# Attention scores over all 128 rows: high and low query halves stacked, or one half beside zeros

## Time and profile before

| What | Value |
|---|---|
| Timed executions | 2894.48, 2897.59, 2910.16 us |
| Profiled execution | 2885.39 us |
| its span | 2883.8 us |
| PE busy | 2633.6 us, 91% |
| PE weight loads | 2125.8 us, 74% |
| DVE busy | 1583.0 us, 55% |
| ACT busy | 1130.1 us, 39% |
| POOL busy | 184.0 us, 6% |
| mean granted TensorE clock | 0.931 |

### The profile page before, as it was taken

How to read it: one execution, slowest core, us unless ns; L and a number is a source line. 1 busy time by engine, 2 the same in 40 slices (tenths; PEclk the granted TensorE clock), 3 DMA queues, 4 the chain that set the end, 5 groups by cost and what they waited for, 6 DMA issues and landing times.

```text
span 2883.8 us, 42857 instructions
## 1 busy us (share of the span) xinstructions
PE 2633.6 (91%) x13598; PEld 2125.8 (74%) x13598; DVE 1583.0 (55%) x3532; ACT 1130.1 (39%) x2388; POOL 184.0 (6%) x221
## 2 busy tenths in 40 slices
PE   1899999989999889999969999998999998799997
PEld 1677777778777667888858677786887786588886
DVE  3456775667266555554244677565745647555522
ACT  1224545354354443222222455453634444322222
POOL 3300000000000220000030000000000011200000
PEclk8979999999999959999987999998999996899998
DMA  4511111212313212333341111122132141133332
GB/s 77 131 30 38 30 45 53 62 55 59 87 45 103 82 29 73 95 96 96 93 108 52 38 38 30 52 59 52 52 88 59 48 135 30 51 95 95 94 99 70
DMA packets 343966, 196.35 MB, mean 68 GB/s; under 512 B 29340, under 2 KB 338704, under 8 KB 343152
## 3 DMA queue, kind: packets, MB, share of 16 engines
q1 hardware_dynamic: 340512, 178.02, 21.6%
q0 software_dynamic: 3280, 16.13, 2.5%
HBM read 186.78 MB, written 7.34 MB: 67 GB/s over the span
## 4 chain that ended last, share of the span: by engine, by line
PE 82%; DVE 7%; issue 4%; DMA 3%; ACT 2%; POOL 1%; DVEq 0%; ACTq 0%; POOLq 0%; SPq 0%
PE acc L1025 60%; PE scores L1025 8%; PE o_acc L1025 6%; PE turn L1167 4%; PE acc L1295 2%; DMA w_f<-in_w_in_dram 1%; DVE trunk L1490 1%; PE scores L1156 1%; DMA head_sink<-in_swa_sinks_dram 1%; ACT w_hi L719 1%; PE scores L1090 1%; DMA w_f<-in_w_out_dram 1%; DVE w_lo L1418 1%; DVE ring L1484 0%; PE scores L1064 0%
## 5 line engine op out<-in xcount | busy, mean ns | idle before, releaser
L1025 PE MATMUL acc<-h_hi,w_hi 128*128 128x512 f32 x1888 | 781.3, 414 | 93.9 <-DVE h_lo L1477 63.6
L1025 PE MATMUL acc<-h_lo,w_hi 128*128 128x512 f32 x1888 | 759.6, 402 | 0.0
L1025 PE MATMUL acc<-h_hi,w_lo 128*128 128x512 f32 x1888 | 758.2, 402 | 0.0
L1418 DVE TENSOR_TENSOR w_lo<-w_f,w_hi 128x1024 fp32r<-128x1024 f32 x336 | 414.3, 1233 | 567.4 <-ACT w_hi L719 565.9
L1025 PEld LDWEIGHTS acc<-h_hi,w_hi 128*128 128x128 f32 x1888 | 364.4, 193 | 208.9 <-issue 84.0
L719 ACT ACTIVATE w_hi<-w_f 128x1024 fp32r<-128x1024 f32 x336 | 353.1, 1052 | 321.6 <-PE acc L1025 278.8
L1025 PEld LDWEIGHTS acc<-h_hi,w_lo 128*128 128x128 f32 x1888 | 364.0, 193 | 82.2 <-issue 3.2
L1025 PEld LDWEIGHTS acc<-h_lo,w_hi 128*128 128x128 f32 x1888 | 365.4, 194 | 71.3 <-issue 2.9
L771 ACT ACTIVATE p_hi<-turn 128x256 fp32r<-128x256 f32 (+4 forms) x416 | 164.0, 394 | 467.5 <-PE turn L1167 466.8
L1516 DVE TENSOR_TENSOR p_lo<-turn,p_hi 128x256 fp32r<-128x256 f32 (+4 forms) x416 | 181.2, 436 | 160.0 <-ACT p_hi L771 156.5
L825 ACT ACTIVATE ring<-ring,neg_max 128x256 f32<-128x256 f32 (+4 forms) x416 | 208.1, 500 | 45.2 <-DVE neg_max L1564 44.4
(11 more groups left out here) (251 smaller groups left out, 3716.2 us busy)
## 6 DMA issues: line engine op xcount, KB each, us to landing
w_f<-in_ffn_w_in_dram SPq DMA_DIRECT2D x88, 512.0 KB, 3.8
w_f<-in_w_gate_dram SPq DMA_DIRECT2D x64, 512.0 KB, 3.6
w_f<-in_w_in_dram SPq DMA_DIRECT2D x62, 512.0 KB, 3.9
w_f<-in_w_branch_dram SPq DMA_DIRECT2D x32, 512.0 KB, 3.4
w_f<-in_ffn_w_out_dram SPq DMA_DIRECT2D x32, 512.0 KB, 3.6
w_f<-in_w_out_dram SPq DMA_DIRECT2D x16, 512.0 KB, 4.7
w_f<-in_ffn_w_out_dram SPq DMA_DIRECT2D x16, 384.0 KB, 3.1
x_spill<-trunk POOLq DMA_DIRECT2D x2, 2048.0 KB, 8.4
```

The lines of the kernel that those rows point to most:

```text
L1025: ins = nc.tensor.matmul(dst, a, b, start=(n == 0 and not added), stop=(n == count - 1))
L1418: nc.vector.tensor_tensor(w_lo[:, u % 2, :], w_f32[:, u % 2, :], w_hi[:, u % 2, :].bitcast(F32), ALU.subtract).then_inc(w_ready, 1)
```

## The change

Queries go to one tile `q_tile` with four slots. MLA uses slots 0 and 1 for high parts, 2 and 3 for low, as before. In the grouped passes each head has a slot of its own (`h % 4`): its high part in the half of the partitions in which its channels lie, its low part in the other half. With keys that lie in both halves, one product over 128 rows gives high and low queries times high keys; a second gives both times low keys (low x low is added by it). In `fox` and `xa` a head keeps its half in a slot for the high and one for the low part, and the other half of these slots is zero, written by POOL once per layer after MLA; its three products contract over 128 rows. The product of the cumulative gate contracts over 128 rows too, so `cum_rows` is filled for its first 40 rows alone. `fox` and `xa` stage by head, eight and four times, the keys of a pair with its first head.

```diff
-ITEMS = [..., ("mla", 8), ("fox", 4), ("xa", 2)]
+ITEMS = [..., ("mla", 8), ("fox", 8), ("xa", XH)]
...
+        q_hi, q_lo = q_tile[:, 0:2, :], q_tile[:, 2:4, :]
...
 # POOL, after the norms of MLA's latents
+                wait_apart(pool, head_done, l * NHD + (HB["mla"] + H + 2))
+                pool.memset(q_tile[HD:P, 0:2, :].bitcast(F32), 0.0).then_inc(q_zero, 1)
+                pool.memset(q_tile[0:HD, 2:4, :].bitcast(F32), 0.0).then_inc(q_zero, 1)
...
 # ACT, stage(n)
+                    elif ps.grouped:
+                        for h in (2 * n, 2 * n + 1):
+                            own = ps.half(h)
+                            ins = nc.scalar.activation(q_tile[own, h % 4, :], buf[own, ps.q_chunk(n), :], ACT.Copy)
+                        ins.then_inc(q_high, 1)
                     else:
-                        if not ps.grouped:
-                            nc.scalar.activation(k_hi[:, n % 2, 0:keys], buf[:, PJ_K[ps.name] + n, 0:keys], ACT.Copy)
-                        nc.scalar.activation(q_hi[:, n % 2, :], buf[:, ps.q_chunk(n), :], ACT.Copy).then_inc(q_high, 1)
+                        if ps is FOX and n < 2:
+                            act.wait_ge(q_zero, l * 2 + 2)
+                        own = ps.half(n)
+                        if n % 2 == 0:
+                            nc.scalar.activation(k_hi[:, n // 2 % 2, 0:keys], buf[:, PJ_K[ps.name] + n // 2, 0:keys],
+                                                 ACT.Copy)
+                        nc.scalar.activation(q_tile[own, 2 * (n % 2), :], buf[own, n // 2, :], ACT.Copy).then_inc(q_high, 1)
...
 # TensorE, score(s)
-                    q = [t[rows, slot, i * P:(i + 1) * P] for t in (q_hi, q_lo)]
-                    k = [t[rows, ps.key_slot(h), k0:k0 + w] for t in (k_hi, k_lo)]
+                    bank, q = scores[s % 2][:, 0:w], slice(i * P, (i + 1) * P)
+                    k = [t[:, ps.key_slot(h), k0:k0 + w] for t in (k_hi, k_lo)]
+                    if ps.grouped:
+                        nc.tensor.matmul(bank, q_tile[:, h % 4, q], k[0], start=True, stop=False)
+                        nc.tensor.matmul(bank, q_tile[:, h % 4, q], k[1], start=False, stop=True).then_inc(scored, 1)
+                        return
+                    at = (h % 2, 2 + h % 2) if ps is MLA else (2 * (h % 2), 2 * (h % 2) + 1)
                     if ps is FOX:
-                        c = slice(rows.start, rows.start + 32 + H)
-                        nc.tensor.matmul(scores[s % 2][:, 0:w], pick[c, h:h + 1].to_broadcast([32 + H, P]),
-                                         cum_rows[c, k0:k0 + w], start=True, stop=False)
-                    first = 1 if ps is FOX else 0
+                        nc.tensor.matmul(bank, pick[:, h:h + 1].to_broadcast([P, P]), cum_rows[:, k0:k0 + w],
+                                         start=True, stop=False)
                     for n in range(3):
-                        product(scores[s % 2][:, 0:w], q, k, n, 3, scored, first)
+                        product(bank, [q_tile[:, a, q] for a in at], k, n, 3, scored, ps is FOX)
...
 # DVE, stage(n)
+                    elif ps.grouped:
+                        for h in (2 * n, 2 * n + 1):
+                            own, other = ps.half(h), ps.half(h + 1)
+                            ins = nc.vector.tensor_tensor(q_tile[other, h % 4, :], buf[own, ps.q_chunk(n), :],
+                                                          q_tile[own, h % 4, :].bitcast(F32), ALU.subtract)
+                        ins.then_inc(qk_ready, 1)
...
 # DVE, before fox
-                for b in range(0, P, 2 * 32):
-                    nc.vector.tensor_copy(cum_rows[b:b + H, :], cum).then_inc(forget, 1)
-                dve.wait_ge(forget, at + 8)
-                for b in range(32, P, 2 * 32):
-                    ins = nc.vector.tensor_tensor(cum_rows[b:b + H, :], cum, cum_rows[0:H, :].bitcast(F32), ALU.subtract)
-                ins.then_inc(forget, 1)
+                nc.vector.tensor_copy(cum_rows[0:H, :], cum).then_inc(forget, 1)
+                dve.wait_ge(forget, at + 7)
+                nc.vector.tensor_tensor(cum_rows[32:32 + H, :], cum, cum_rows[0:H, :].bitcast(F32),
+                                        ALU.subtract).then_inc(forget, 1)
```

More of the change, by code:

```diff
@@ L93 @@
 TB, NTN = offsets(TURNS)
-ITEMS = [("cmp", 4), ("sel", 4), ("win", 4), ("swa", 4), ("mla", 8), ("fox", 4), ("xa", 2)]
+ITEMS = [("cmp", 4), ("sel", 4), ("win", 4), ("swa", 4), ("mla", 8), ("fox", 8), ("xa", XH)]
 IB, NIT = offsets(ITEMS)
@@ L198, in item, with half @@
     def item(self, h):
-        if self.name == "mla":
-            return h, h % 2, slice(0, P)
-        return h // 2, (h // 2) % 2, slice(h % 2 * HD, (h % 2 + 1) * HD)
+        return h // 2 if self.grouped else h
+    def half(self, h):
+        return slice(h % 2 * HD, (h % 2 + 1) * HD)
     def key_slot(self, h):
-        return h // (H // KVH) if self.grouped else self.item(h)[1]
+        if self.grouped:
+            return h // (H // KVH)
+        return h % 2 if self.name == "mla" else h // 2 % 2
     def staged_at(self, n):
@@ L309, in build @@
             v_lo = sb("v_lo", [P, NT, BW], F32R, st)
-            q_hi = sb("q_hi", [P, 2, S], F32R, st)
-            q_lo = sb("q_lo", [P, 2, S], F32R, st)
+            q_tile = sb("q_tile", [P, 4, S], F32R, st)
             k_hi = sb("k_hi", [P, 2, S], F32R, st)
@@ L354, in build @@
         qk_ready = sem("qk_ready")
+        q_zero = sem("q_zero")
         kg_high = sem("kg_high")
@@ L944, in _ @@
                 project(l, "fox", lambda c, r_: proj[:, bass.ds(r_ + c, 1), :], table=1)
-                act.wait_ge(forget, l * 9 + 2)
+                act.wait_ge(forget, l * 8 + 2)
                 nc.scalar.activation(exp_neg, logit, ACT.Exp, scale=-1.0).then_inc(forget_act, 1)
@@ L1147, in score @@
                     k0, w = ps.keys(i)
-                    item, slot, rows = ps.item(h)
                     if i == 0:
-                        pe.wait_ge(qk_ready, l * NIT + (IB[ps.name] + item + 1))
+                        pe.wait_ge(qk_ready, l * NIT + (IB[ps.name] + ps.item(h) + 1))
                     pe.wait_ge(biased, st + (s + 1))
-                    q = [t[rows, slot, i * P:(i + 1) * P] for t in (q_hi, q_lo)]
-                    k = [t[rows, ps.key_slot(h), k0:k0 + w] for t in (k_hi, k_lo)]
+                    bank, q = scores[s % 2][:, 0:w], slice(i * P, (i + 1) * P)
[5 more added lines that the diff above has]
+                    at = (h % 2, 2 + h % 2) if ps is MLA else (2 * (h % 2), 2 * (h % 2) + 1)
                     if ps is FOX:
-                        c = slice(rows.start, rows.start + 32 + H)
-                        nc.tensor.matmul(scores[s % 2][:, 0:w], pick[c, h:h + 1].to_broadcast([32 + H, P]),
-                                         cum_rows[c, k0:k0 + w], start=True, stop=False)
-                    first = 1 if ps is FOX else 0
+                        nc.tensor.matmul(bank, pick[:, h:h + 1].to_broadcast([P, P]), cum_rows[:, k0:k0 + w],
+                                         start=True, stop=False)
                     for n in range(3):
-                        product(scores[s % 2][:, 0:w], q, k, n, 3, scored, first)
+                        product(bank, [q_tile[:, a, q] for a in at], k, n, 3, scored, ps is FOX)
                 def turn_probs(s):
@@ L1549, in stage @@
                                                 k_hi[0:HD, n % 2, :].bitcast(F32), ALU.subtract)
[L1550 to L1554, removed]
+                        nc.vector.tensor_tensor(q_lo[:, n % 2, :], proj[:, n, :], q_hi[:, n % 2, :].bitcast(F32),
+                                                ALU.subtract).then_inc(qk_ready, 1)
+                    elif ps.grouped:
[4 more added lines that the diff above has]
+                        ins.then_inc(qk_ready, 1)
+                    else:
+                        own = ps.half(n)
+                        if n % 2 == 0:
+                            k = n // 2 % 2
+                            nc.vector.tensor_tensor(k_lo[:, k, 0:keys], buf[:, PJ_K[ps.name] + n // 2, 0:keys],
+                                                    k_hi[:, k, 0:keys].bitcast(F32), ALU.subtract)
+                        at = 2 * (n % 2)
+                        nc.vector.tensor_tensor(q_tile[own, at + 1, :], buf[own, n // 2, :],
+                                                q_tile[own, at, :].bitcast(F32), ALU.subtract).then_inc(qk_ready, 1)
                 def bias_scores(s):
@@ L1825, in _ @@
                 project(l, "fox")
-                at = l * 9
+                at = l * 8
                 nc.vector.tensor_scalar(cum, narrow[R_F:R_F + H, :], f_bias[:, bass.ds(l, 1)], None,
```

## The result

| | before | after |
|---|---|---|
| Timed executions, median (range), us | 2896.03 (2893.88 to 2910.16) | 2856.47 (2852.38 to 2857.30) |
| Profiled execution, us | 2885.39 | 2857.30 |
| its span, us | 2883.8 | 2855.6 |
| mean granted clock | 0.931 | 0.911 |

There are four timed executions of each kernel in the comparison. The ratio is 0.9854 (95% interval 0.9824 to 0.9885): 1.5% or 40 us faster, where 102 us were forecast and 2768 was the low, 2824 the high end of the range. The mean granted clock of the four executions after is 0.911 to 0.915, so the profiled one is no exception.

A forecast was written before the change was run, and what follows sets the result against it. TensorE was taken as the bound (82% of the chain of waits), with DVE taking over in WIN and near in SEL. Pass gains less start costs summed to 51.2 us a layer, 102.4 in all: 2783.0 profiled, 2795 median, range 2768 to 2824.

The forecast's parts named there:

- The reading of TensorE's spacing: All passes with 64-row scores: going from 128 rows to 64 and back costs a step 0.33 us.
- the rival of products only: Spacing comes from o_acc's 64 columns and stays; only removed products gain, 14.3 us a layer, 2869 us; chance 0.07.
- The rival without a DVE limit: SEL and WIN follow TensorE's own time, 10.5 us a layer more gained, 2774 us; chance 0.14.
- DVE needs 1.99 + 0.09: SWA step: DVE's busy time plus the added subtraction, under the 2.64 us forecast, so TensorE stays full.
- The rival of the rising clock: XA's clock rises with full rows, DVE bounds its step at about 1.6 us, 2786 us; within the forecast's 0.75.
- The starts: First scores of passes: SEL, WIN and SWA wait 0.69 us more each, FOX gains 1.1 us.
- DVE (1.20) is far off: CMP step: DVE's 1.20 us is no limit, so 0.27 us a step is gained over 27 steps, 7.3 us.
- In CMP the filler ahead covers it: CMP's start: the added subtraction before the first score is hidden by filler and costs nothing.
- The +0.69: Start of SEL, WIN and SWA: q_lo becomes two subtractions behind two ACT copies, 0.69 us more each.
- The slower rival: With one product less and DVE stalls, the clock falls in CMP, SEL and WIN; up to 3057 us; chance 0.03.
- with one product less: Condition in the clock-fall case for CMP, SEL and WIN: fewer TensorE products, with DVE stalls, lower the granted clock.
- the half of a switch: CMP step: half of 0.33 us taken for the row switch, plus 0.11 for one product, 0.27 in all.

The follow-up runs named there:

- the last experiment: Kernel staged by head in all grouped passes, with the second product of SWA's scores issued twice; 2776.27 us in one execution, against 2773.79 without it.
- taking the meeting away: Changed kernel with CMP's second pair of heads staged at step 3 instead of step 0; 2786.58 us, ratio to before 0.9643.
- the run with halved staging: Kernel before, products untouched, CMP's queries staged by halves with two copies and two subtractions per pair; 2917.22 us against 2889.33 before.

## Why the prediction was wrong, step by step

**The reading of TensorE's spacing was right.** FOX isolates it (the same four products, the first over 128 rows instead of 40 and the others over 128 instead of 64): the step went from 3.121 to 2.795 us, 0.326 where 0.33 was taken. PE's timeline of one FOX step after, keys 256 wide:

```profile
824.93 0.22 PE L1042 MATMUL o_acc<-p_hi,v_lo 128*64 128x128 f32 x1
824.99 0.33 PE L1176 MATMUL scores<-cum_rows,pick 128*128 128x256 f32 x1
825.16 0.28 PE L1042 MATMUL scores<-k_hi,q_tile 128*128 128x256 f32 x1
825.28 0.28 PE L1042 MATMUL scores<-k_lo,q_tile 128*128 128x256 f32 x1
825.40 0.28 PE L1042 MATMUL scores<-k_hi,q_tile 128*128 128x256 f32 x1
825.52 0.40 PE L1042 MATMUL acc<-h_hi,w_hi 128*128 128x512 f32 x1
825.75 0.40 PE L1042 MATMUL acc<-h_lo,w_hi 128*128 128x512 f32 x1
```

The starts lie 0.06, 0.17, 0.12, 0.12, 0.12 and 0.23 us apart, MLA's numbers of the earlier trace rows and not the 0.16, 0.22, 0.21 and 0.33 of the earlier trace rows. That excludes the rival of products only. MLA stayed at 2.63.

**SEL and WIN were right in kind.** DVE took over: 2.17 and 2.05, forecast 2.10 and 2.07. The rival without a DVE limit is excluded, as TensorE is busy for 33.46 of 34.72 and 30.62 of 32.80 us and all its waits in these two windows are for DVE's division or low part of the probabilities.

**SWA was 0.06 a step short**, 2.70 for 2.64. "DVE needs 1.99 + 0.09" compared rates: on the mean DVE had time to spare, in the steps where staging follows a weight split it had not. A single product is worth 0.10 there, as the last experiment shows, and one step of 3.7 us among 16 of 2.64 makes (3.7 - 2.64)/16 = 0.07, which is about the difference.

**XA took the other branch.** The step is 1.60 us, the forecast's 1.89 had the lower clock. The rival of the rising clock had said 1.6 with DVE as the bound, and TensorE's waits in the window (2.1 us) are all for DVE.

**The starts.** SWA's first score waits 4.37 us instead of 3.59 (0.78 more, 0.69 taken), FOX's 3.12 instead of 4.37 (1.25 less, 1.1 taken). SEL's wait became shorter (0.42 for 0.93), and WIN's first score, which did not wait in layer 0 before, waits 2.31 us, where 0.69 was taken.

**The failed step is "DVE (1.20) is far off", by which CMP's doubled subtraction was put at nothing, with "In CMP the filler ahead covers it" beside it.** The +0.69 was set against the first score of a pass only, where for CMP it held, since TensorE does not wait there; otherwise it was spread over the steps as 0.09, and in CMP not even that. The item that counted is the second one, `stage(1)` at step 0: no filler covers it, since the transposes for which TensorE waits stand behind the filler of step 0, and DVE comes to them after a weight split and both subtractions. Shown: this wait is 0.22, 1.03, 1.30, 1.78 and 2.03 us in five kernels, and the clock of CMP fell right behind the last two only, in both layers; between 1.35 and 1.78 us nothing was measured; taking the meeting away gives the clock back (2786.58 us), and putting a 2.03 us wait into the kernel before takes it away (2967.34 us).

The slower rival had named the event, a clock that falls in CMP after DVE stalls, with a chance of 0.03; and against it stood that CMP held 1.00 in the trace. That only told that nothing had disturbed it. The size was right: 1.72 times the step was priced, and 3.15/1.80 = 1.75 is measured against the same products at 1.00. But the rival was drawn as all or nothing over three passes, and "with one product less" is not needed, as the run with a longer wait in the kernel before shows. WIN and SEL stayed at 1.00 in their middles although TensorE waited in them.

**The sum closes.** The forecast for the profiled execution was 2783.0 us and it took 2857.3, so 74.3 are to be found. Forecast for CMP's two passes was 56.7 + 56.8 - 14.6 = 98.9, and they took 171.6: 72.7. The rest, 1.6 us, is small partly by luck: over both layers SEL is 5.2 us and SWA 3.4 above the forecast, MLA 0.4, and the stretches between the passes 3.6, while XA is 6.1, FOX 2.6 and WIN 2.3 below it. With the clock held, CMP gains 5.1 us a pass and not 7.3 (step 1.80, not 1.71; 1.77 when staged by head): the half of a switch taken there was too much.

**Left open.** What brings the clock back, and why a wait lowers it in one pass and not in another. CMP did not come back from 0.50 in any run in which it fell, with four or five filler products a step and TensorE busy throughout, whereas SWA and FOX, whose passes begin with stretches at the lower level, return within 7 us in the kernels before and after, and within 17 in the run with halved staging. In XA the runs show one thing that changes it, the rows: back after 7 us with 128, not at all with 64. That is no rule for CMP, which stayed down with 128. Nor do the runs say why WIN and FOX ran longer at the lower level in the kernel before with halved staging.

## What to carry to other kernels

When an edit doubles a short operation, price it where it stands, not as a rate: find the step in which its engine is already late, and follow what waits there. A wait of TensorE of about 2 us deserves a look at the granted clock behind it: in CMP 1.81 us more of waiting cost the pass 40.6 us, while in WIN waits as long cost 7 us at the lower level or none. And products over half the rows between products over all of them are dear here not for themselves but for the spacing around them.

## What the chip showed that was not expected

- A pass whose TensorE is busy 100% of the time can stay at 1.2 GHz to its end (CMP, 3.15 us a step for 85.7 us; 3.47 us and 97.3 with the old products), though the same work runs at 2.4 GHz where nothing disturbed it (1.80 and 1.98).
- Zeros in the other half of the rows made XA faster beyond their spacing: the clock of its middle is 0.92 with 128 rows and 0.50 with 64, 1.60 against 2.19 us a step, and putting the 64 rows back alone brings 0.50 and 2.19 back.
- A copy or subtraction of 512 columns takes as long on 64 partitions as on 128 (0.69 against 0.68 us on DVE, 0.63 against 0.62 on ACT), so that splitting one by halves doubles it.
